# Feed-forward of a hybrid decoder block: up-projection by Strassen's seven half-size products, activations through DRAM, down-projection with half its weight held in SBUF

## The chip, the cores and the metric

One core of a Trainium2 chip runs the whole kernel. TensorE (PE), VectorE (DVE), ScalarE (ACT), GpSimd (POOL) and SyncE (SP, which here only issues DMAs) run side by side and wait for each other by semaphores. The metric is device time in microseconds for one execution.

## What is computed

A decoder block on 2048 positions of width 1024: an S5 state-space head group and eight stick-breaking attention heads, an output projection, cross-attention over 256 memory tokens, and a feed-forward of inner width 4096. The two parts that matter here:

```python
def block(qi, i):   # stick_breaking_attention, per block of 128 queries
    logits = einsum('bqhd,bkhd->bhqk', qi, k) * scale
    log_beta = log_sigmoid(logits)
    log_1m_beta = where(mask, log_sigmoid(-logits), 0.0)
    after = lax.cumsum(log_1m_beta, axis=3, reverse=True) - log_1m_beta
    w = where(mask, exp(log_beta + after), 0.0)
    return einsum('bhqk,bkhd->bqhd', w, v)
...
h = rmsnorm(x, g_mlp[l])                                   # (2048, 1024)
x = x + jnp.square(jax.nn.relu(h @ w_up[l])) @ w_down[l]    # w_up 1024 x 4096, w_down 4096 x 1024
```

All is float32. For the large products each operand is kept as a rounded part (hi, fp32r, made by ACT) and the rest (lo, made by DVE), and three matmuls, hi x hi, hi x lo and lo x hi, stand for one.

## The kernel before

`decoder_block` calls one function for each stage, and a barrier of all engines ends each.

**Feed-forward (`mlp`).** The rows are cut into 2 chunks of 1024 (`CHUNKS2`), the inner width into 16 blocks of 256 (`BLOCKS`, `FB`). For a chunk h^T (1024 x 1024) lies in SBUF as `ht_hi` and `ht_lo`. It is made by norm on DVE (`norm_x`), 8 transposes per tile of 128 rows on PE (`turn_h`), `high_h` on ACT and `low_h` on DVE. For each block `up` makes four units (two halves of rows by two tiles of 128 inner columns), each of 24 matmuls of 128x128 by 512 columns (lines 2687 to 2689). ACT takes Relu out of PSUM, DVE multiplies it by itself (line 2612), ACT rounds to `a_hi`, DVE subtracts to `a_lo`. `down` follows one block behind: 8 tiles of 128 rows, each of 12 such matmuls, 6 for each half of the output columns (lines 2703 to 2705), and DVE adds each tile from PSUM to `y` in SBUF (line 2595). The weights of a block come in one DMA of 1 MB each (`load_up`, line 2449, and `load_down`), into one buffer each (`up_raw`, `down_raw`), and are split by `split_up` and `split_down` on ACT and DVE. POOL only makes the identity matrix. At a chunk's end `boundary` finishes the last block and turns the tiles of the next chunk. Most of the blocks run in hardware loops (`Fori`).

The order on each engine is written out by hand: `program` runs prologue, up, down and boundary, and a `Tally` counts steps in a semaphore.

**Stick-breaking (`stick_breaking`).** Heads go in pairs. For each tile of 128 queries `score` (lines 796 to 799) makes the logits on PE, ACT the two sigmoids, DVE the running product (scan, line 740), POOL the weights (line 690), PE turns them (811) and multiplies by v (828). At the start SP runs `load_half(0, 0)`: q of both heads for 1024 positions (2 DMAs of 512 KB), hi and lo part of k, each twice (8 DMAs of 256 KB), then v. The first score waits for all ten.

## Time and profile before

| what | us |
|---|---|
| runs shown: median of 3 (lowest to highest) | 3311.54 (3311.31 to 3315.63) |
| the profiled execution's own time | 3312.09 |
| its span, first to last instruction | 3310.3 |
| feed-forward stage: first instruction to end of span | 1848.8 to 3310.3 |
| attention stage: first instruction to last score | 642.8 to 1174 |

"Busy" is the time in which an engine had an instruction under way. Matmuls overlap, so that one of 392 ns starts every 0.2267 us; that distance is the pace. "Idle before, releaser" is the time in which the engine stood still ahead of the instruction, and what ended it. PEclk is the granted clock of PE as a share of the full one; a mean share between the two levels says how long each of them held. The chain of work that ended last is followed back from the end of the span. In the names f_ is the feed-forward, a_ the attention, s_ the state-space stage, p_ the input projection.

### The profile page before, as it was taken

The numbers are of one execution on the slowest core, as the hardware profiler recorded it, in microseconds if no ns is written. First come the engines' busy times: TensorE is split into PE (matmuls) and PEld (weight loads), VectorE is DVE, ScalarE is ACT, GpSimd is POOL, SyncE is SP. The second block draws the span as 40 slices with busy tenths as digits, with TensorE's granted clock in tenths as the row PEclk, the third lists the DMA queues.
The fourth block names the chain that finished last, engine by engine and source line by source line (L and its number), as shares of the span: only waits on it lengthen the run. The fifth ranks groups of instructions, "written<-read, shape, count | busy, mean of one in ns | idle before, by whom it ended". The sixth has DMA issues, their size and how long they took to land. (4 is left out here: it accounts for less than half of the span.)

```text
span 3310.3 us, 42553 instructions
## 1 busy us (share of the span) xinstructions
PE 3008.5 (91%) x15810; PEld 2545.5 (77%) x15810; DVE 1717.8 (52%) x2404; ACT 1106.8 (33%) x1839; POOL 494.4 (15%) x397
## 2 busy tenths in 40 slices
PE   6999936599999969986999699999999999999998
PEld 5888824488988957764888588888887788888887
DVE  5333257587877855436565444444444544444444
ACT  4333215376766752213343221111111211111111
POOL 1212113455555532110000000000000000000000
PEclk9999967899999989997999899999999999999999
DMA  4232252362242033324222521111111411111111
GB/s 163 83 92 73 77 79 43 86 167 55 49 101 54 11 80 102 95 93 155 71 85 69 202 65 51 50 38 51 42 47 52 165 51 38 51 51 51 51 38 64
DMA packets 230220, 251.36 MB, mean 76 GB/s; under 512 B 107457, under 2 KB 181185, under 8 KB 230081
## 3 DMA queue, kind: packets, MB, share of 16 engines
q1 hardware_dynamic: 230096, 249.74, 25.8%
q8 instruction: 75, 1.23, 0.2%
q14 instruction: 49, 0.39, 0.0%
HBM read 189.79 MB, written 58.73 MB: 75 GB/s over the span
## 5 line engine op out<-in xcount | busy, mean ns | idle before, releaser
L2595 DVE TENSOR_TENSOR f_y<-f_ps_down,f_y 128x1024 f32<-128x1024 f32 x256 | 313.2, 1224 | 324.9 <-PE f_ps_down L2705 324.8
L2538 ACT ACTIVATE f_act_f<-f_ps_up 128x512 f32<-128x512 f32 x128 | 76.5, 598 | 1032.0 <-PE f_ps_up L2689 1032.0
L2687 PE MATMUL f_ps_up<-f_ht_hi,f_up_hi 128*128 128x512 f32 x1024 | 401.2, 392 | 6.4 <-DVE f_act_f L2612 6.4
L2703 PE MATMUL f_ps_down<-f_down_hi,f_a_hi 128*128 128x512 f32 x1024 | 400.4, 391 | 6.1 <-issue 6.1
L2688 PE MATMUL f_ps_up<-f_ht_lo,f_up_hi 128*128 128x512 f32 x1024 | 400.4, 391 | 0.0
L2689 PE MATMUL f_ps_up<-f_ht_hi,f_up_lo 128*128 128x512 f32 x1024 | 400.3, 391 | 0.0
L2705 PE MATMUL f_ps_down<-f_down_hi,f_a_lo 128*128 128x512 f32 x1024 | 400.0, 391 | 0.0
L2704 PE MATMUL f_ps_down<-f_down_lo,f_a_hi 128*128 128x512 f32 x1024 | 400.0, 391 | 0.0
L690 POOL TENSOR_TENSOR a_w<-a_on,a_left 128x640 f32<-128x640 f32 (+5 forms) x192 | 282.1, 1469 | 254.6 <-DVE a_left L740 114.6
L2612 DVE SCALAR_TENSOR_TENSOR f_act_f<-f_ps_up,f_act_f 128x512 f32<-128x512 f32 x128 | 88.5, 691 | 395.3 <-ACT f_act_f L2538 395.3
L828 PE MATMUL a_ps_y<-a_wt,a_v 128*96 128x128 f32 x2176 | 270.6, 274 | 5.2 <-DVE a_yt L763 5.2
L828 PEld LDWEIGHTS a_ps_y<-a_wt,a_v 128*96 128x96 f32 x2176 | 249.6, 164 | 5.8 <-issue 5.8
L740 DVE TENSOR_TENSOR_SCAN a_left<-a_ps_z,a_one 128x896 f32<-128x896 f32 (+7 forms) x128 | 207.3, 1620 | 77.5 <-ACT a_ps_z L702 75.9
L2687 PEld LDWEIGHTS f_ps_up<-f_ht_hi,f_up_hi 128*128 128x128 f32 x1024 | 193.6, 189 | 47.0 <-DVE f_ht_lo L2578 6.8
L2703 PEld LDWEIGHTS f_ps_down<-f_down_hi,f_a_hi 128*128 128x128 f32 x1024 | 193.3, 189 | 46.8 <-issue 6.7
L2689 PEld LDWEIGHTS f_ps_up<-f_ht_hi,f_up_lo 128*128 128x128 f32 x1024 | 193.4, 189 | 40.5
L2688 PEld LDWEIGHTS f_ps_up<-f_ht_lo,f_up_hi 128*128 128x128 f32 x1024 | 193.6, 189 | 40.2
L2705 PEld LDWEIGHTS f_ps_down<-f_down_hi,f_a_lo 128*128 128x128 f32 x1024 | 193.2, 189 | 40.4
L2704 PEld LDWEIGHTS f_ps_down<-f_down_lo,f_a_hi 128*128 128x128 f32 x1024 | 193.1, 189 | 40.2
L701 ACT ACTIVATE a_on<-a_ps_z 128x640 f32<-128x640 f32 (+5 forms) x192 | 148.8, 775 | 162.6 <-PE a_ps_z L799 120.8
L796 PE MATMUL a_ps_z<-a_k_hi,a_q 128*128 128x512 f32 (+3 forms) x392 | 145.3, 378 | 30.6 <-DMA a_k_lo<-k 22.7
L485 PE MATMUL p_acc<-p_w_hi,p_ht_hi 128*128 128x512 f32 x384 | 155.7, 405 | 2.7 <-DVE p_ht_lo L390 2.7
(352 smaller groups left out, 5505.9 us busy)
## 6 DMA issues: line engine op xcount, KB each, us to landing
f_up_raw<-in_w_up SPq DMA_DIRECT2D x32, 1024.0 KB, 5.3
f_down_raw<-in_w_down SPq DMA_DIRECT2D x32, 1024.0 KB, 4.8
p_xt<-in_x SPq DMA_DIRECT2D x16, 512.0 KB, 4.8
q<-p_qt SPq DMA_DIRECT2D x16, 512.0 KB, 3.2
k<-p_qt SPq DMA_DIRECT2D x16, 512.0 KB, 3.2
a_q<-q SPq DMA_DIRECT2D x16, 512.0 KB, 5.6
a_k_hi<-k SPq DMA_DIRECT2D x32, 256.0 KB, 8.4
...
```

The lines of the kernel that those rows point to most:

```text
L485: pe.matmul(out, ht_hi[b][:, k, rows], w_hi[:, k, cols], start=(k == 0), stop=False)
L690: pool.tensor_tensor(w[m % WS][:, 0:k1 - k0], on[m % ONS][:, 0:k1 - k0], left[a][i % 2][:, at + k0 + 1:at + k1 + 1], ALU.mult).then_inc(we ...
L701: act.activation(on[m % ONS][:, 0:k1 - k0], z, ACT.Sigmoid, scale=SCALE).then_inc(sig_on, 1)
L740: dve.tensor_tensor_scan(left[a][i % 2][:, at + k0:at + k1][:, ::-1], z_ps[m % 2][:, 0:k1 - k0][:, ::-1], one[:, 0:1].to_broadcast([P, k1 ...
L828: mm = pe.matmul(y_ps[a][0:TALL, 0:P], v[a][(2 * s + half) % 3][:, cols], wt[m % WTS][:, t, :], start=(first and t == 0), stop=(last and t ...
L2595: dve.tensor_tensor(y[:, t, :], down_ps[t % 2][:, :], y[:, t, :], ALU.add).then_inc(added.sem, 1)
L2687: pe.matmul(o, up_hi[:, k, cols], ht_hi[:, k, rows], start=(k == 0), stop=False)
L2688: pe.matmul(o, up_hi[:, k, cols], ht_lo[:, k, rows], start=False, stop=False)
L2689: mm = pe.matmul(o, up_lo[:, k, cols], ht_hi[:, k, rows], start=False, stop=(k == KC - 1))
L2703: pe.matmul(o, a_hi[par][:, s, rows], down_hi[:, s, cols], start=(s == 0), stop=False)
L2704: pe.matmul(o, a_hi[par][:, s, rows], down_lo[:, s, cols], start=False, stop=False)
L2705: mm = pe.matmul(o, a_lo[par][:, s, rows], down_hi[:, s, cols], start=False, stop=(s == S - 1))
```

## The change

**Up-projection.** A chunk of 1024 rows and a block of 256 inner columns, at depth 1024, is one product of 2 x 2 by 2 x 2 quarters. It is done with seven products of quarter operands (Strassen's scheme in Winograd's form) instead of eight: each of 12 matmuls of 128x128 by 512, into one PSUM bank. Their operands are quarters of W (A11 to A22) and of h (H11 to H22), or sums of them. For each block POOL makes the four weight sums S1 to S4, ACT rounds and DVE subtracts all seven weight operands; for each chunk the seven h operands (T1 to T4 among them, made by DVE for chunk 0 and by POOL for chunk 1) lie in SBUF as hi and lo, one buffer each. DVE puts the results together from PSUM (C11, U2, U3, C21, C22, U4, C12) in an order woven with its subtractions for the next block. ACT applies Relu, then Square, and SP stores the activations to a DRAM tensor `a` (4096 x 2048). There is one raw buffer for the up weights, as before. The norm of x goes to ACT, and g is multiplied in by DVE when it copies the turned tile from PSUM. The tiles of chunk 1 are turned in blocks 1 to 8, one each.

**Down-projection.** It starts after all 32 blocks. For each half of the output columns the whole depth of `w_down` (32 tiles, hi and lo) lies in SBUF; for each group of 512 rows the sum over the depth of 4096 stays in four PSUM banks, in two sets by turns. A step is one depth tile: 12 matmuls. Activations are loaded back, two depth tiles per 512 KB DMA, split by ACT and DVE into a ring of 3; in the first group of each half the weights are loaded and split beside them. `y` is added once per group. All 256 steps are written out.

**Attention's start.** The loads of the first pair's lower half are cut at column 512: ten loads of 0 to 511, then v, then ten loads of 512 to 1023. The first score waits for the first ten, query tile 4 for the second ten.

The diff, cut to its core:

```diff
-            load_half(0, 0)
+            def load_begin(cols, done_q, done_k):
+
+                for a in range(2):
+                    sp.dma_start(q2[a][:, cols].bitcast(F32), q_dram[a, :, cols]).then_inc(done_q, DMA)
+                    for dst, part in ((k2_hi[a][0], 0), (k2_lo[a][0], 1)):
+                        for copy in range(2):
+                            sp.dma_start(dst[copy * HEAD:(copy + 1) * HEAD, cols].bitcast(F32),
+                                         k_dram[a, part * HEAD:(part + 1) * HEAD, cols]).then_inc(done_k, DMA)
+
+            load_begin(slice(0, BANK), begin_loaded, begin_loaded)
+            for a in range(2):
+                sp.dma_start(v[a][0][:, 0:BLOCKS * HEAD // 2].rearrange("p (i d) -> p i d", d=HEAD),
+                             v_dram[0:HALF, a * HEAD:(a + 1) * HEAD].rearrange("(i p) d -> p i d", p=P)
+                             ).then_inc(v_loaded[0], DMA)
+            load_begin(slice(BANK, HALF), q_loaded[0], k_loaded[0])
             load_half(0, 1)
...
-                if i in (0, BLOCKS // 2) and first:
+                if s == 0 and i == 0:
+                    pe.wait_ge(begin_loaded, 10 * DMA)
+                elif i == (BANK // P if s == 0 else 0) or i == BLOCKS // 2 and first:
                     half = i // (BLOCKS // 2)
...
+        big = sb("big", [P, 35, 1024], F32R)
+        h_raw = sb("h_raw", [P, KC, ROWS])
+        w_raw = sb("w_raw", [P, 2, 1024])
+        w_sum = sb("w_sum", [P, 3, KH, P])
+        u2 = sb("u2", [P, BANK])
+        xr = sb("xr", [P, 4, 1024])
...
+        def hv(i, low):
+            return big[:, 4 * i + 2 * low:4 * i + 2 * low + 2, :].rearrange("p a (b q) -> p (a b) q", b=2)
+
+        def wv(i, low):
+            return big[:, 28 + i, low * BANK:(low + 1) * BANK].rearrange("p (k q) -> p k q", q=P)
...
+        W_SRC = {ONE: A11, SIX: S2, TWO: A12, SEVEN: S3, FIVE: S1, FOUR: A22, THREE: S4}
+        W_SUMS = {FIVE: 1, SIX: 2, SEVEN: 3, THREE: 4}
+        H11, H12 = h_raw[:, :KH, :BANK], h_raw[:, :KH, BANK:]
+        H21, H22 = h_raw[:, KH:, :BANK], h_raw[:, KH:, BANK:]
+        T3, T2, T4, T1 = H12, H11, H21, H12
+        H_SRC = {ONE: H11, SIX: T2, TWO: H21, SEVEN: T3, FIVE: T1, FOUR: T4, THREE: H22}
+        H_SUMS = {SEVEN: 1, SIX: 2, FOUR: 3, FIVE: 4}
...
+        BOUNDARY = {(BLOCKS - 1, 1): ONE, (BLOCKS - 1, 3): TWO, (BLOCKS - 1, 4): SIX, (BLOCKS - 1, 5): SEVEN,
+                    (BLOCKS - 1, 6): THREE, (BLOCKS, 0): FOUR, (BLOCKS, 2): FIVE}
+
+        def boundary_variant(b, slot, plain):
+            return None if plain else BOUNDARY.get((b, slot))
+
+        STEPS = [(half, g, k) for half in range(2) for g in range(GROUPS) for k in range(FF_TILES)]
...
             def load_up(b):
...
+                sp.dma_start(raw, w_up[:, b * FB:(b + 1) * FB].rearrange("(k p) f -> p k f", p=P)).then_inc(w_loaded, DMA)
...
+            def body(b, chunk):
+                if b < LAST:
+                    sp.wait_ge(w_low.sem, w_low.at(b, FOUR + 1))
+                    sp.wait_ge(w_summed.sem, w_summed.at(b, 4))
+                    load_up((b + 1) % BLOCKS)
+                if b == 0:
+                    load_x(TILES)
+                    load_x(TILES + 1)
+                if is_turning(b, False) and TILES + b + 1 < 2 * TILES:
+                    load_x(TILES + b + 1)
+                store_a(b, chunk, SQ11, 0, 0, 0)
+                if b == LAST:
+                    load_down(0)
+                    for i in range(4):
+                        sp.wait_ge(stored[i].sem, stored[i].at(BLOCKS - 1, DMA))
+                    load_a(0)
+                    load_down(1)
+                    load_a(1)
+                store_a(b, chunk, SQ21, 3, 1, 0)
+                store_a(b, chunk, SQ22, 2, 1, 1)
+                store_a(b, chunk, SQ12, 1, 0, 1)
...
+            def sum_one(b):
+                pool.wait_ge(w_loaded, b * DMA + DMA)
+                pool.wait_ge(w_low.sem, w_low.at(b - 1, FIVE + 1))
+                pool.tensor_tensor(S1, A21, A22, ALU.add).then_inc(w_summed.sem, 1)
+
+            def sum_two(b):
+                pool.wait_ge(w_summed.sem, w_summed.at(b, 1))
+                pool.wait_ge(w_low.sem, w_low.at(b - 1, THREE + 1))
+                pool.tensor_tensor(S2, S1, A11, ALU.subtract).then_inc(w_summed.sem, 1)
+
+            def sum_three(b):
+                pool.wait_ge(w_low.sem, w_low.at(b - 1, SEVEN + 1))
+                pool.tensor_tensor(S3, A11, A21, ALU.subtract).then_inc(w_summed.sem, 1)
+
+            def sum_four(b):
+                pool.wait_ge(w_low.sem, w_low.at(b, SIX + 1))
...
+            def high_w(b, i):
+                act.wait_ge(made.sem, made.at(b - 1, i + 1))
+                if i in W_SUMS:
+                    act.wait_ge(w_summed.sem, w_summed.at(b, W_SUMS[i]))
+                else:
+                    act.wait_ge(w_loaded, b * DMA + DMA)
+                act.activation(wv(i, 0), W_SRC[i], ACT.Copy).then_inc(w_high.sem, 1)
...
+            def activate(b, r, made_by, n):
+                act.wait_ge(combined.sem, combined.at(b, made_by))
+                act.activation(r, r, ACT.Relu).then_inc(relued.sem, 1)
+                act.wait_ge(relued.sem, relued.at(b, n))
+                act.activation(r, r, ACT.Square).then_inc(squared.sem, 1)
...
+            def body(b, plain=False):
+                more = plain or b < LAST
+                act.wait_ge(made.sem, made.at(b, ONE + 1))
+                act.wait_ge(combined.sem, combined.at(b - 1, C12))
+                act.activation(u2[:, :], PS_A, ACT.Copy).then_inc(one_copied.sem, 1)
+                if more:
+                    high_w(b + 1, ONE)
+                slot_end(b, 0, plain)
+                if more:
+                    high_w(b + 1, TWO)
+                slot_end(b, 1, plain)
+                activate(b, R11, C11, SQ11)
...
+            def high_a(n):
+                m = n // 2
+                act.wait_ge(a_loaded[m % 2], (m // 2 + 1) * DMA)
+                if n < RING:
+                    act.wait_ge(made.sem, made.at(LAST, FOUR + n + 1))
+                else:
+                    act.wait_ge(step_made, n - RING + 1)
+                act.activation(a_slot(n, 0), a_raw(m)[:, n % 2, :], ACT.Copy).then_inc(a_high, 1)
+
+            for n, (half, g, k) in enumerate(STEPS):
+                high_a(n)
+                if g == 0:
+                    high_down(half, k)
...
+            def body(b, plain=False):
+                more = plain or b < LAST
+                if more:
+                    low_w(b + 1, ONE)
+                slot_end(b, 0, plain)
+                dve.wait_ge(made.sem, made.at(b, TWO + 1))
+                dve.wait_ge(one_copied.sem, one_copied.at(b, 1))
+                dve.wait_ge(stored[0].sem, stored[0].at(b - 1, DMA))
+                dve.tensor_tensor(R11, PS_B, u2[:, :], ALU.add).then_inc(combined.sem, 1)
...
+            def add_group(group):
+                dve.wait_ge(y_loaded[group % 2], (group // 2 + 1) * 4 * DMA)
+                for t in range(4):
+                    dve.wait_ge(step_made, (group + 1) * FF_TILES)
+                    dve.tensor_tensor(y_tile(group, t), acc(group, t), y_tile(group, t), ALU.add).then_inc(added, 1)
...
+            def product(b, i, plain):
+                pe.wait_ge(w_low.sem, w_low.at(b, i + 1))
+                if not plain and b % BLOCKS == 0:
+                    pe.wait_ge(hv_low, b // BLOCKS * PRODUCTS + HV_ORDER.index(i) + 1)
+                o = OUT_BANK[i]
+                for k in range(KH):
+                    pe.matmul(o, wv(i, 0)[:, k, :], hv(i, 0)[:, k, :], start=(k == 0), stop=False)
+                    pe.matmul(o, wv(i, 0)[:, k, :], hv(i, 1)[:, k, :], start=False, stop=False)
+                    mm = pe.matmul(o, wv(i, 1)[:, k, :], hv(i, 0)[:, k, :], start=False, stop=(k == KH - 1))
+                mm.then_inc(made.sem, 1)
...
+            def body(b, plain=False):
+                pe.wait_ge(combined.sem, combined.at(b - 1, C21))
+                product(b, ONE, plain)
+                pe.wait_ge(combined.sem, combined.at(b - 1, U4))
+                product(b, TWO, plain)
+                if not plain and b == 0:
+                    for n in range(TILES - 2, TILES):
+                        turn_h(n)
+                pe.wait_ge(combined.sem, combined.at(b - 1, C12))
+                product(b, SIX, plain)
+                pe.wait_ge(combined.sem, combined.at(b - 1, U3))
+                product(b, SEVEN, plain)
+                pe.wait_ge(one_copied.sem, one_copied.at(b, 1))
+                product(b, FOUR, plain)
+                if is_turning(b, plain):
+                    turn_h(TILES - 1 + b)
+                pe.wait_ge(combined.sem, combined.at(b, C11))
+                product(b, FIVE, plain)
+                pe.wait_ge(combined.sem, combined.at(b, U2))
+                product(b, THREE, plain)
...
+            for n, (half, g, k) in enumerate(STEPS):
+                group = half * GROUPS + g
+                if k == 0:
+                    if group == 0:
+                        pe.wait_ge(h_copied, 2 * TILES)
+                    elif group == 1:
+                        pe.wait_ge(combined.sem, combined.at(LAST, C12))
+                    else:
+                        pe.wait_ge(added, (group - 1) * 4)
+                pe.wait_ge(a_low, n + 1)
+                if g == 0:
+                    pe.wait_ge(down_low, half * FF_TILES + k + 1)
+                for t in range(4):
+                    o = acc(group, t)
+                    rows = slice(t * P, (t + 1) * P)
+                    hi, lo = (a_slot(n, low)[:, rows] for low in range(2))
+                    pe.matmul(o, hi, w_slot(k, 0), start=(k == 0), stop=False)
+                    pe.matmul(o, hi, w_slot(k, 1), start=False, stop=False)
+                    mm = pe.matmul(o, lo, w_slot(k, 0), start=False, stop=(k == FF_TILES - 1))
+                mm.then_inc(step_made, 1)
```

## Rows read from the trace of the kernel before

**Rows 1.** The page, busy us (share of the span) and instructions of each engine

```profile
PE 3008.5 (91%) x15810; PEld 2545.5 (77%) x15810; DVE 1717.8 (52%) x2404; ACT 1106.8 (33%) x1839; POOL 494.4 (15%) x397
```

**Rows 2.** The page, chain that ended last, by line, share of the span

```profile
PE f_ps_up L2687 7%; PE f_ps_down L2703 7%; PE f_ps_up L2688 7%; PE f_ps_up L2689 7%; PE f_ps_down L2705 7%; PE f_ps_down L2704 7%; PE f_ps_th L2663 0%; DVE f_ht_lo L2578 0%; DVE f_xt L2571 0%; DMA f_g_row<-in_g_mlp 0%; ACT f_ht_hi L2515 0%; DVE f_y L2595 0%; DVE f_up_lo L2583 0%; DVE f_act_f L2612 0%; PE f_ps_down L2663 0%
```

**Rows 3.** Busy us by stretch (PE, PEld, DVE, ACT, POOL), clock, DMA share, GB/s

```profile
1848.80:1874.20 25.40, 8.29 (x40) 7.29 (x41) 16.25 (x24) 5.88 (x6) 0.46 (x2) 0.57 0.72 251
1874.20:1900.00 25.80, 22.48 (x101) 18.55 (x100) 9.77 (x10) 6.53 (x9) 0.00 (x0) 0.89 0.68 246
...
2000.00:2100.00 100.00, 100.00 (x443) 82.81 (x442) 45.70 (x48) 20.64 (x30) 0.00 (x0) 1.00 0.15 53
...
2557.00:2614.00 57.00, 46.55 (x218) 37.81 (x218) 33.80 (x31) 12.44 (x14) 0.00 (x0) 0.91 0.54 203
...
3305.10:3310.30 5.20, 0.19 (x1) 0.00 (x0) 1.23 (x1) 0.00 (x0) 0.00 (x0) 0.97 0.42 169
```

**Rows 4.** Groups of instructions, feed-forward: count, busy us, mean ns, idle before

```profile
L2687 PE MATMUL f_ps_up<-f_ht_hi,f_up_hi 128*128 128x512 f32 x1024 | 401.2, 392 | 6.4 <-DVE f_act_f L2612 6.4
...
L2595 DVE TENSOR_TENSOR f_y<-f_ps_down,f_y 128x1024 f32<-128x1024 f32 x256 | 313.2, 1224 | 324.9 <-PE f_ps_down L2705 324.8
...
L2612 DVE SCALAR_TENSOR_TENSOR f_act_f<-f_ps_up,f_act_f 128x512 f32<-128x512 f32 x128 | 88.5, 691 | 395.3 <-ACT f_act_f L2538 395.3
L2620 DVE TENSOR_TENSOR f_a_lo<-f_act_f,f_a_hi 128x512 fp32r<-128x512 f32 x128 | 87.5, 684 | 4.2 <-ACT f_a_hi L2546 4.2
L2546 ACT ACTIVATE f_a_hi<-f_act_f 128x512 fp32r<-128x512 f32 x128 | 79.6, 622 | 6.3 <-DVE f_act_f L2612 6.3
...
L2521 ACT ACTIVATE f_up_hi<-f_up_raw 128x1024 fp32r<-128x1024 f32 x64 | 67.4, 1053 | 0.0
```

**Rows 5.** Instructions in order: start us, us, engine, line [idle before]

```profile
2000.14 0.39 PE L2687 MATMUL f_ps_up<-f_ht_hi,f_up_hi 128*128 128x512 f32 x1
...
2013.74 0.39 PE L2703 MATMUL f_ps_down<-f_down_hi,f_a_hi 128*128 128x512 f32 x1
...
2013.94 0.60 ACT L2538 ACTIVATE f_act_f<-f_ps_up 128x512 f32<-128x512 f32 x1 [3.38 <-PE f_ps_up L2689]
```

**Rows 6.** Pieces of the chain that ended last: start us, us, what

```profile
2572.15 0.87 PE f_ps_th L2663 x8
...
3281.68 0.47 PE f_ps_down L2703
```

**Rows 7.** Instructions of DVE in order, feed-forward's opening and last block

```profile
1857.62 2.48 DVE L2571 SCALAR_TENSOR_TENSOR f_xt<-f_xt,f_stat,f_g_row 128x1024 f32<-128x1024 f32 x2
...
3286.29 1.22 DVE L2595 TENSOR_TENSOR f_y<-f_ps_down,f_y 128x1024 f32<-128x1024 f32 x1 [4.71 <-PE f_ps_down L2705]
```

**Rows 8.** Line 2449: SP's issue of the up weights, ns; landing, us

```profile
L2449 SPq DMA_DIRECT2D f_up_raw<-in_w_up x32: 368/368/1017, 1851.7 to 3172.1; - x32
...
DMA to landing us min/median/max: 5.1/5.3/10.3
```

**Rows 9.** DVE and POOL in order, state-space stage, 628 to 634 us

```profile
628.84 1.26 POOL L1011 TENSOR_TENSOR s_s_cos<-s_tables,s_sigma 128x510 f32<-128x510 f32 x1 [2.79 <-DVE s_sigma L1291]
629.20 1.44 DVE L1299 TENSOR_TENSOR s_s_sin<-s_tables,s_sigma 128x510 f32<-128x510 f32 x1
...
631.85 0.69 DVE L1299 TENSOR_TENSOR s_s_sin<-s_tables,s_sigma 128x510 f32<-128x510 f32 x1
631.95 1.71 POOL L1011 TENSOR_TENSOR s_s_cos<-s_tables,s_sigma 128x510 f32<-128x510 f32 x1 [1.85 <-issue]
```

**Rows 10.** Groups of POOL's instructions: a 128x512 product

```profile
L270 POOL TENSOR_TENSOR p_qn<-p_qn,p_gq_row 128x512 f32<-128x512 f32 x32 | 40.6, 1292 | 304.8 <-DVE p_qn L418 304.8
```

**Rows 11.** Instructions in order at attention's start

```profile
642.80 0.83 SPq L638 DMA_DIRECT2D a_q<-q  x2
...
660.45 0.44 PE L796 MATMUL a_ps_z<-a_k_hi,a_q 128*128 128x128 f32 x1 [22.73 <-DMA a_k_lo<-k]
```

**Rows 12.** Busy us by stretch after attention's start, columns as in rows 3

```profile
680.00:700.00 20.00, 19.87 (x154) 17.79 (x155) 18.45 (x22) 15.35 (x26) 13.21 (x8) 1.00 0.97 293
```

More of the change, by code:

```diff
@@ L2354, in mlp @@
     FB = 256
-    S = FB // P
     BLOCKS = D_FF // FB
-    HALVES = ROWS // BANK
-    U = HALVES * S
-    XT = 4
-    LAST = CHUNKS2 * BLOCKS - 1
+    ALL = CHUNKS2 * BLOCKS
+    LAST = ALL - 1
+    KH = KC // 2
+    ONE, TWO, SIX, SEVEN, FOUR, FIVE, THREE = range(7)
+    PRODUCTS = 7
+    HV_ORDER = (ONE, TWO, SIX, SEVEN, THREE, FOUR, FIVE)
+    FF_TILES = D_FF // P
+    GROUPS = SEQ // BANK
+    RING = 3
     with ExitStack() as ctx:
@@ L2384, in mlp @@
         ident = sb("ident", [P, P])
+        g_col = sb("g_col", [P, KC])
         stat = sb("stat", [P, 4, SEQ // P])
-        up_ps = [ps(f"up{i}", [P, BANK]) for i in range(2)]
-        down_ps = [ps(f"down{i}", [P, D_MODEL]) for i in range(2)]
-        th_ps = ps("th", [P, KC, P])
+        bank = [ps(f"bank{i}", [P, BANK]) for i in range(4)]
+        th_ps = [ps(f"th{i}", [P, KC, P]) for i in range(2)]
+        PS_A, PS_B, PS_C, PS_D = (b[:, :] for b in bank)
+        OUT_BANK = {ONE: PS_A, TWO: PS_B, SIX: PS_C, SEVEN: PS_D, FOUR: PS_A, FIVE: PS_B, THREE: PS_C}
@@ L2417, in turned_into @@
[L2417 to L2437 removed]
+        h_copied = sem("h_copied")
@@ L2505, in _ @@
+            sums(0)
+            sums(1)
+            for b in range(1, BLOCKS - 1):
+                sums(b + 1)
+            sum_heads(SEVEN)
+            sum_one(BLOCKS)
+            sum_two(BLOCKS)
+            sum_heads(SIX)
+            sum_three(BLOCKS)
+            sum_heads(FOUR)
+            sum_four(BLOCKS)
+            sum_heads(FIVE)
+            for b in range(BLOCKS, LAST):
+                sums(b + 1)
         @block.scalar
         def _(act):
-            for t in (up_high, down_high, relued, a_high):
+            for t in (w_high, one_copied, relued, squared):
@@ new lines, in low_h @@
+            def low_h(chunk, i):
+                dve.wait_ge(hv_high, chunk * PRODUCTS + HV_ORDER.index(i) + 1)
+                dve.tensor_tensor(hv(i, 1), H_SRC[i], hv(i, 0).bitcast(F32), ALU.subtract).then_inc(hv_low, 1)
+            for n in range(4):
+                copy_h(n)
+            low_h(0, ONE)
+            low_w(0, ONE)
+            copy_h(4)
+            low_h(0, TWO)
+            low_w(0, TWO)
+            copy_h(5)
+            low_w(0, SIX)
+            low_w(0, SEVEN)
+            copy_h(6)
@@ new lines, in _ @@
+            low_w(0, FOUR)
+            low_w(0, FIVE)
+            copy_h(7)
+            low_w(0, THREE)
+            dve.wait_ge(h_copied, TILES)
+            dve.tensor_tensor(T3, H22, H12, ALU.subtract).then_inc(h_summed[0], 1)
+            dve.wait_ge(h_summed[0], H_SUMS[SEVEN])
+            dve.wait_ge(hv_low, HV_ORDER.index(ONE) + 1)
+            dve.tensor_tensor(T2, T3, H11, ALU.add).then_inc(h_summed[0], 1)
+            low_h(0, SIX)
+            low_h(0, SEVEN)
+            dve.wait_ge(h_summed[0], H_SUMS[SIX])
@@ new lines, in _, with slot_end @@
+            dve.wait_ge(hv_low, HV_ORDER.index(TWO) + 1)
+            dve.tensor_tensor(T4, H21, T2, ALU.subtract).then_inc(h_summed[0], 1)
+            low_h(0, THREE)
+            dve.wait_ge(hv_low, HV_ORDER.index(SEVEN) + 1)
+            dve.tensor_tensor(T1, H22, T2, ALU.subtract).then_inc(h_summed[0], 1)
+            for i in (FOUR, FIVE):
+                low_h(0, i)
+            def slot_end(b, slot, plain):
+                i = boundary_variant(b, slot, plain)
+                if i is not None:
+                    low_h(1, i)
```

563 lines of the change are left out of this document (294 added, 269 removed).

## The prediction

> **What bounds the kernel now.** I read the shares of the page first, then the chain that ended last, then stretches of the feed-forward, then single instructions. TensorE (PE) is busy 91% of the span [rows 1], and the six feed-forward matmul groups alone hold 43% of it in the chain [rows 2]. In a stretch amid the feed-forward PE is busy 100.00 of 100 us at granted clock 1.00, while DVE is busy 45.70 and ACT 20.64 [rows 3]. So there only fewer or faster matmuls help. Sixty matmuls pass from 2000.14 to 2013.74, 0.2267 us each [rows 5]. The stage runs from 1848.8 to the end of the span at 3310.3: 1461.5 us. Its 6144 matmuls take 1392.8 of them; 68.7 are opening, chunk boundary and end [rows 3].
>
> **Fewer products.** Up-projection: 32 blocks of 7 products of 12 matmuls, 2688, where there were 3072; down: 256 steps of 12, 3072 as before. 5760 x 0.2267 = 1305.8 us, 87.0 less. Every matmul keeps its form (128x128 by 512), so I take the pace unchanged, in the down part too. One product lasts 2.72 us, one block 19.04. Everything else the change does costs time, or is to be hidden in those 19.04 us.
>
> **One steady block.** Let t = 0 be the first matmul of product ONE. Per block DVE has 7 subtractions of 0.684 and 8 sums of 0.691, 10.3 us; ACT 15 instructions of about 0.62, 9.4 us [rows 4]; POOL 4 sums of 1.27 (a 128x512 product took 1.292) [rows 10], 5.1 us. Each fits. What may not fit is the loop through the single raw weight buffer. SP issues load_up(b+1) behind the last store of block b-1, which waits for its last Square. THREE's result is seen 0.2 us after its end (PE 2013.74, ACT 2013.94) [rows 5]; sum 0.69, Relu and Square 1.3, two issues 0.45: the load is issued at 2.6. Landing takes a median 5.3, least 5.1, most 10.3 [rows 8]. Now 256 KB stores go just ahead; at 251 GB/s [rows 3] one takes 1 us, so I estimate L = 6.2. ACT's and DVE's first conversions for the next block stand in their queues ahead of this block's sums, so until the data lands both queues stand still; PE misses nothing until FIVE at 13.6, which needs C11.
> After landing at Z, POOL's four sums meet DVE's subtractions. Where both read SBUF they take turns: DVE's L1299 takes 0.69 alone, but 1.44 when it starts 0.36 us into a POOL sum, ending 0.54 after it; a POOL sum started while DVE runs takes 1.71 instead of 1.26 [rows 9]. Laid out in turns: subtraction ONE ends at Z+1.9, C11 Z+2.5, subtraction TWO Z+3.65, SIX Z+5.35, SEVEN Z+7.2, C21 Z+7.85. From there ACT: Relu+Square 1.3, conversion FIVE 0.5, Relu+Square 1.3, conversion THREE 0.5, Relu+Square 1.3, then the issues 0.45: the next load can go at Z+13.2. The loop is L + 13.2 = 19.4 us, against PE's 19.04. It costs 0.4; I take 0.5 in each of the 21 blocks that have nothing else, 10.5 us. Bounds: nothing (if L is below 5.8), or 1.8 if one more POOL sum of 1.27 falls into the loop.
> The Trainium skill (SBUF — State Buffer, Who interferes with whom) speaks against this use of POOL: a VectorE instruction with two SBUF inputs and a GpSimd one that reads SBUF exclude each other for the whole instruction. By that rule the loop is the 19.4 above; without it the same chain would be L + 12.0 = 18.2, hidden. The pairs at 629 and 632 us agree with the rule.
>
> **Opening.** Up to the first norm nothing changes much: 8.8 us (DVE 1857.62) [rows 7]; the nine small loads take the place of one of g. Then DVE must do 8 copies of 1.22, 7 weight subtractions of 0.69, 4 sums and 7 subtractions of 2048 columns before block 0 can end. A 2048-column instruction is 0.69 + 3 x 0.53 = 2.3 (0.53 is the difference between 1024 and 512 columns) [rows 4]. That is 39.9 us. First norm and transposes 3.1, DVE's waits for ACT and PE by a schedule laid out by hand 12.7, then a subtraction and C11 1.4 and products FIVE and THREE 5.4: block 1 starts at 71.4, and I add 3 for matmuls at the low clock. After a gap a step of 12 takes 4.4 us (3281.68 to the add at 3286.29, less 0.2) instead of 2.72 [rows 6, 7], 1.7 more. 74.4 less block 0's own 19.0 leaves 55.4. If the waits halve it is 48.
>
> **Turning the second chunk** in blocks 1 to 8: 0.87 of transposes each [rows 6], as before the change too. Here PE waits between FOUR and FIVE for the norm, which stands in ACT's queue behind the conversions of loaded weights: norm ends about 14.6, FOUR ended at 13.6. 0.87 + 1.0 = 1.9 each, 15.2. The loop's 0.4 is hidden in it.
>
> **Chunk boundary**, blocks 15 and 16. Each of the 7 operands of h has one buffer, so it is replaced between its product in block 15 and that in block 16: 7 x (2.0 ACT, twice a 1024-column one, + 2.3 DVE), and POOL's three chained sums of about 5 us. DVE's load over the two blocks is 2 x 10.3 + 16.1 = 36.7 of 38.1, in a fixed order with POOL's sums. ONE(16) waits for C21(15), which is behind the operand conversions: near t = 25 instead of 19, 5.7 lost. TWO and SIX lose some more; FOUR(16) waits for its operand, which ACT makes only after load_up(17) has landed, 6.6; FIVE about 4.3. In all 19.5, plus 3 for the low clock, plus 5 for turns with POOL: 27.5. Bounds: 12, if the waits overlap, and 40.
>
> **Into down, and down itself.** After the last product: sum, Relu, Square, then conversion and subtraction of the first activation and weight slots, 4.3 us, plus 1.7 at the low clock: 6. Then in each 2.72 us step ACT has one or two instructions of 0.62, DVE one or two of 0.68; with weights DMA brings 1 MB in 5.44 us, 190 GB/s, below the 251 of [rows 3], and five steps of lead less 2.7 of conversions leave 7.9 us for a landing. The four sums of a group run beside three ready steps. I cost the reading of activations at nothing; the cover is the ring of 3. If the landing took 10.3, the 32 loads with weights would lose up to 2.4 each, 77 us: unlikely, since they go two at a time. 3072 matmuls stay 696.4. The store and load instructions that pass SP at a group change (8 x 0.4) lie in that lead too. End: four adds of 0.65, issue and landing, 6.0 where it was 5.2 [rows 3].
>
> Sum for the stage: 1305.8 + 55.4 + 15.2 + 10.5 + 27.5 + 6 + 6 = 1426.4, against 1461.5: 35.1 saved. Of 87.0 more than half is given back.
>
> **Attention's start.** PE's first score starts at 660.45, after waiting for DMA; loads are issued from 642.80 [rows 11]. That is 3.15 MB of q and k in 17.65 us, 178 GB/s. The change lets the first four query tiles start after half: 8.8 us earlier. The second half, behind v, makes 3.67 MB or 20.6 us, about when tile 4 wants it (its score started some 11 us after the first). From 680 PE is full (19.87 of 20) [rows 12], so a lead stays. Against it: ten more issues of about 0.6 us on SP ahead of the upper half, at a DMA share of 0.97. Bounds -2 to 8.8; I take 7, nearest to the landing row.
>
> **Forecast.** 35.1 + 7 = 42.1. The profiled execution took 3312.09 (span 3310.3, 1.8 around it), 0.55 above the median 3311.54 of the runs shown: 3312.1 - 42.1 = 3270.
>
> **Rivals.**
> A. The weight loop is hidden and the boundary's waits overlap: 10.5 + 15.5 less, 3244. For it: 5.3 as median landing, and DVE and ACT over half idle. Against: stores now go just ahead of each load.
> B. The weight loop is 1.3 us longer (one more turn with POOL): 21 x 1.3 = 27, 3297; with half of it 3283. For it: the pairs [rows 9] and the fixed order of POOL's sums.
> C. Slower than before: the loop sets the pace outright. With a period P the loss is 21 x (P - 19.04) + 8 x (P - 20.9); my sum without it saves 52.6, so from P = 21.4 the kernel is no faster, and from 21.6 (L = 8.4) it is slower by over 0.2%. At the longest landing seen, 10.3, P is 23.5: 3374. For it: single buffer, and each queue in order. Against: that 10.3 had four 512 KB loads ahead of it.
> D. The attention part does nothing, since the saturated DMA only passes the wait on: 3277. For it: DMA share 0.97 afterwards [rows 12].
>
> **Chances.** Forecast, 3258 to 3280: 0.42; A 0.20; B 0.22 (3283 to 3300); C 0.06; D 0.10. The bounds of the opening and boundary reach 20 either way. 3242 to 3296 leaves out C and the ends of A and B, about 2 in 10. A measurement here can tell about 0.2% (6.6 us) from no change. Faster 0.91, within 0.03, slower 0.06.
>
> **What would show it.** Steps right: 2688 up matmuls at 0.2267; a steady block of 19.0 to 19.6 (more: B or C, and then PE's idle time sits before the product that needs C11 or C12); landing of the up weights near 6; DVE subtractions of more than 0.69 beside POOL sums; about 75 us from the stage's start to block 1; a gap of 20 to 35 around blocks 15 and 16; a down part of 696 without gaps; first score about 9 us after the stage's start. Wrong: gaps inside the down steps, a pace above 0.227, or a first score as late as before.

## The result, and the profile after

The changed kernel takes 3293.38 us (median of 5 runs, 3291.99 to 3293.99) against 3311.54 before (3307.62 to 3315.63): ratio 0.9942, interval 0.9928 to 0.9957. It is 18.2 us faster. I had forecast 41.5 us, a time of 3270 with 3242 to 3296 as range. The time lies near the upper end of the range, beside rival B and not beside the forecast.

The page of the kernel after: busy time of each engine, and by line the chain that ended last.

```profile
PE 2946.1 (90%) x15426; PEld 2485.3 (76%) x15426; DVE 1696.0 (52%) x2566; ACT 1362.9 (41%) x2301; POOL 705.0 (21%) x529
...
PE f_ps_th L3001 4%; PE f_ps_th L3003 4%; PE f_ps_th L3002 4%; PE f_ps_bank L3002 4%; PE f_ps_bank L3001 4%; PE f_ps_bank L3003 4%; DMA f_w_raw<-in_w_up 2%; PE f_ps_bank L2957 1%; PE f_ps_bank L2959 1%; PE f_ps_bank L2958 1%; ACT f_xr L2713
```

In [rows 2] the up-projection held 21% of the chain and DMA nothing. Now the down part still holds its share (21% before, six groups of 4% now), but the up-projection's matmuls (L2957 to L2959) hold 1% each: the chain runs beside them, through the load of raw up weights (2%, some 66 us) and ACT's Relu (L2713). This is what a loop through another engine looks like in a chain. The stage starts at 1841.8 and the span ends at 3291.5. Busy time of its stretches, columns as in [rows 3]: opening, blocks 1 to 8 (which turn the second chunk), plain blocks 9 to 13, the chunk boundary, plain blocks 17 to 31, and down:

```profile
1841.80:1911.70 69.90, 36.49 (x149) 30.43 (x150) 49.08 (x49) 31.23 (x33) 13.54 (x10) 0.69 0.33 109
1911.70:2103.20 191.50, 172.06 (x737) 141.04 (x737) 93.97 (x122) 87.22 (x139) 47.05 (x32) 0.94 0.35 106
2103.20:2201.70 98.50, 97.33 (x427) 79.66 (x426) 53.22 (x70) 45.00 (x78) 29.54 (x20) 1.00 0.33 104
2224.60:2290.70 66.10, 45.53 (x157) 35.12 (x158) 49.68 (x37) 32.56 (x41) 27.43 (x11) 0.79 0.21 64
2290.70:2582.70 292.00, 288.58 (x1261) 235.31 (x1259) 155.70 (x204) 135.16 (x234) 82.73 (x56) 1.00 0.36 111
2587.00:3285.00 698.00, 698.00 (x3072) 577.57 (x3072) 230.01 (x346) 192.82 (x317) 0.00 (x0) 1.00 0.42 140
```

Most of the idle time beyond opening and boundary is in the second row: 19.4 us without a matmul in 8 blocks, and a granted clock of 0.94. What PE waited for there (total us, times, longest us), and then the instructions of one such block in order:

```profile
PE f_ps_th L2945 <- ACT f_xr L2692: 19.4, 8, 2.9
```

```profile
1963.39 0.38 SPq L2527 DMA_DIRECT2D f_w_raw<-in_w_up  x1
...
1970.30 1.29 POOL L2631 TENSOR_TENSOR f_w_sum<-f_w_raw 128x512 f32<-128x512 f32 x1 [17.75 <-DMA f_w_raw<-in_w_up]
...
1970.32 1.15 ACT L2700 ACTIVATE f_big<-f_w_raw 128x512 fp32r<-128x512 f32 x2 [6.27 <-DMA f_w_raw<-in_w_up]
...
1975.62 1.13 ACT L2692 ACTIVATE f_xr<-f_xr,f_stat 128x1024 f32<-128x1024 f32 x1
...
1976.80 1.97 PE L2945 MATMUL f_ps_th<-f_ident,f_xr 128*128 128x128 f32 x8 [2.52 <-ACT f_xr L2692]
...
1978.42 0.78 PE L2957 MATMUL f_ps_bank<-f_big 128*128 128x512 f32 x1
...
1987.59 0.38 SPq L2527 DMA_DIRECT2D f_w_raw<-in_w_up  x1
```

The load issued at 1963.39 is in at 1970.30. ACT converts two weight blocks, makes four more instructions and then, at 1975.62, the norm (L2692); PE, idle for 2.52 us, turns the tile from 1976.80 to 1978.42 (1.62 us), and product FIVE begins, slow at first. The next load goes out at 1987.59, 17.3 us after the landing. The next block therefore finds its weights as late as this one did: the delay is not absorbed, it sets the period, 24.2 us here.

The same links in a plain block: load issued, landed, a subtraction of DVE, POOL's third sum, and the next issue:

```profile
2352.25 0.38 SPq L2527 DMA_DIRECT2D f_w_raw<-in_w_up  x1
2358.96 1.15 ACT L2700 ACTIVATE f_big<-f_w_raw 128x512 fp32r<-128x512 f32 x2 [6.68 <-DMA f_w_raw<-in_w_up]
...
2359.63 1.22 DVE L2816 TENSOR_TENSOR f_big<-f_w_raw,f_big 128x512 fp32r<-128x512 f32 x1 [8.29 <-ACT f_big L2700]
...
2361.95 1.74 POOL L2640 TENSOR_TENSOR f_w_sum<-f_w_raw 128x512 f32<-128x512 f32 x1
...
2371.97 0.38 SPq L2527 DMA_DIRECT2D f_w_raw<-in_w_up  x1
```

L is 6.7, the rest 13.0, the period 19.7. Over all 32 loads the landing has (min/median/max):

```profile
DMA to landing us min/median/max: 6.1/6.6/8.8
```

### The profile page after: what moved, and what is told of

The parts are those of the page before. It is cut to its first block and busy times, and to the rows that moved or that the text cites. A ratio compares the mean times of both kernels' runs of the same rounds, so it can differ in the third digit from the quotient of the medians.

```text
span 3291.5 us, 42858 instructions
## 1 busy us (share of the span) xinstructions
PE 2946.1 (90%) x15426; PEld 2485.3 (76%) x15426; DVE 1696.0 (52%) x2566; ACT 1362.9 (41%) x2301; POOL 705.0 (21%) x529
## 5 line engine op out<-in xcount | busy, mean ns | idle before, releaser
L2917 DVE TENSOR_TENSOR f_big<-f_h_raw,f_big 128x512 fp32r<-128x512 f32 x256 | 177.0, 691 | 463.3 <-ACT f_big L2792 463.3
L2957 PE MATMUL f_ps_bank<-f_big 128*128 128x512 f32 x896 | 361.1, 403 | 43.8 <-DVE f_big L2820 19.8
L2792 ACT ACTIVATE f_big<-f_h_raw 128x512 fp32r<-128x512 f32 x256 | 161.7, 632 | 497.9 <-PE f_ps_bank L3003 259.7
L2958 PE MATMUL f_ps_bank<-f_big 128*128 128x512 f32 x896 | 356.5, 398 | 0.0
L2959 PE MATMUL f_ps_bank<-f_big 128*128 128x512 f32 x896 | 356.0, 397 | 0.0
L2957 PEld LDWEIGHTS f_ps_bank<-f_big 128*128 128x128 f32 x896 | 173.9, 194 | 89.2 <-issue 25.1
L2816 DVE TENSOR_TENSOR f_big<-f_w_raw,f_big 128x512 fp32r<-128x512 f32 x96 | 103.5, 1078 | 244.3 <-ACT f_big L2700 244.3
L3001 PE MATMUL f_ps_th<-f_big 128*128 128x512 f32 x512 | 200.0, 391 | 4.0 <-DVE f_big L2912 4.0
L2959 PEld LDWEIGHTS f_ps_bank<-f_big 128*128 128x128 f32 x896 | 172.8, 193 | 37.3
L2958 PEld LDWEIGHTS f_ps_bank<-f_big 128*128 128x128 f32 x896 | 173.6, 194 | 35.6
L3003 PE MATMUL f_ps_th<-f_big 128*128 128x512 f32 x512 | 199.8, 390 | 0.0
L3002 PE MATMUL f_ps_th<-f_big 128*128 128x512 f32 x512 | 199.8, 390 | 0.0
L3001 PE MATMUL f_ps_bank<-f_big 128*128 128x512 f32 x512 | 199.2, 389 | 0.0
L3002 PE MATMUL f_ps_bank<-f_big 128*128 128x512 f32 x512 | 199.2, 389 | 0.0
L3003 PE MATMUL f_ps_bank<-f_big 128*128 128x512 f32 x512 | 199.2, 389 | 0.0
```

Source lines behind the costliest of these rows:

```text
L2792: act.activation(a_slot(n, 0), a_raw(m)[:, n % 2, :], ACT.Copy).then_inc(a_high, 1)
L2917: dve.tensor_tensor(a_slot(n, 1), a_raw(n // 2)[:, n % 2, :], a_slot(n, 0).bitcast(F32), ALU.subtract).then_inc(a_low, 1)
L2957: pe.matmul(o, wv(i, 0)[:, k, :], hv(i, 0)[:, k, :], start=(k == 0), stop=False)
L2958: pe.matmul(o, wv(i, 0)[:, k, :], hv(i, 1)[:, k, :], start=False, stop=False)
L2959: mm = pe.matmul(o, wv(i, 1)[:, k, :], hv(i, 0)[:, k, :], start=False, stop=(k == KH - 1))
L3001: pe.matmul(o, hi, w_slot(k, 0), start=(k == 0), stop=False)
```

## The experiments

**The theory.** The up-projection is paced by one loop: load, landing, conversions, Relu and Square, store, next load. In plain blocks it is slightly longer than PE's 19.04 us; in turning blocks it also passes through the norm, the transposes and product FIVE, and is 24 us. **Rivals:** the norm's place in ACT's queue alone costs the gap; POOL's turns with DVE do; or the landing is slow for a reason of its own. I measured block lengths from one copy of product ONE (ACT, out of PSUM) to the next: the mean of blocks 1 to 8 for a turning block, of blocks 17 to 30 for a plain one. "Boundary" is blocks 15 and 16 together, in us:

| kernel | median | ratio (interval) | turning block | plain block | boundary |
|---|---|---|---|---|---|
| after | 3293.38 | 0.9942 (0.9928 to 0.9957) | 23.94 | 19.6 | 66.1 |
| load two stores earlier | 3247.27 | 0.9804 (0.9787 to 0.982) | 20.01 | 19.04 | 64.1 |
| norm earlier | 3268.98 | 0.9869 (0.9851 to 0.9887) | 20.68 | 19.6 | 65.7 |
| small POOL sums | 3258.89 | 0.9838 (0.9821 to 0.9854) | 21.38 | 19.04 | 64.6 |
| a quarter of each load | 3244.42 | 0.9799 (0.9782 to 0.9815) | 19.99 | 19.04 | 61.0 |
| before, attention's part alone | 3304.72 | 0.9979 (0.997 to 0.9988) | - | - | - |
| load and norm earlier | 3247.53 | 0.9807 (0.9792 to 0.9822) | 19.96 | 19.04 | 62.4 |
| load earlier, boundary sums on DVE | 3239.37 | 0.9784 (0.9769 to 0.9799) | 19.96 | 19.04 | 58.0 |
| all of these, and a new order | 3234.32 | 0.9768 (0.9753 to 0.9783) | 19.88 | 19.04 | 52.4 |

Ratios are to the kernel before, run beside each.

**Load earlier.** SP issues the load for block b+2 behind the second of block b's four stores, no longer behind the fourth:

```diff
-                if b < LAST:
-                    sp.wait_ge(w_low.sem, w_low.at(b, FOUR + 1))
-                    sp.wait_ge(w_summed.sem, w_summed.at(b, 4))
-                    load_up((b + 1) % BLOCKS)
...
                 store_a(b, chunk, SQ21, 3, 1, 0)
+                if b + 2 < ALL:
+                    sp.wait_ge(w_low.sem, w_low.at(b + 1, FOUR + 1))
+                    sp.wait_ge(w_summed.sem, w_summed.at(b + 1, 4))
+                    load_up((b + 2) % BLOCKS)
```

> The changed kernel with one edit on SP: the up weights of a block are loaded as soon as their buffer is free, two stores earlier in SP's queue, instead of behind the last store of the block before. Loop theory (the pace is set by the round trip load, conversions, last Square, last store, next load: 13.1 us after landing in a plain block, 17.3 in a turning block, plus 6.6 of landing): with the load off the round trip a plain block falls from 19.66 to 19.04 and a turning block from 23.9 to about 19.9, FOUR(16) no longer waits for its load; 3293.4 - 13 - 31 - 5 = about 3245. Turns theory (POOL and DVE excluding each other is itself the limit, wherever the load lands): plain blocks stay at 19.5 or more, total above 3275. Transposes theory (turning blocks are long by PE's transposes and the low clock alone): turning blocks stay above 22, total about 3278.

It came as the loop said: 3247.27. Turning blocks are 19.04 + 1.0, plain ones 19.04. Two stretches, turning blocks and plain blocks 17 to 31, columns as above:

```profile
1913.50:2073.60 160.10, 159.73 (x738) 132.64 (x737) 91.71 (x122) 88.89 (x139) 46.89 (x32) 1.00 0.43 130
...
2251.80:2535.00 283.20, 283.20 (x1251) 234.52 (x1250) 148.77 (x203) 146.21 (x232) 82.33 (x56) 1.00 0.36 112
```

PE has one gap of 0.37 us left in them, and the clock is 1.00 in both. The loads themselves are no faster, yet it doesn't matter, since each has a lead:

```profile
DMA to landing us min/median/max: 5.7/7.0/8.8
```

No work was taken away: one DMA issue stands elsewhere in SP's queue, and that is worth 46.1 us, more than twice what the whole change brought.

**Norm earlier.** ACT's norm of a turning block goes ahead of the conversions that wait for loaded weights:

```diff
                 act.activation(u2[:, :], PS_A, ACT.Copy).then_inc(one_copied.sem, 1)
+                if is_turning(b, plain):
+                    norm_x(TILES - 1 + b)
...
-                if is_turning(b, plain):
-                    norm_x(TILES - 1 + b)
                 if more:
                     high_w(b + 1, FOUR)
```

> The changed kernel with one edit on ACT: in the turning blocks the norm stands at the start of the block, ahead of the conversions that wait for the load. Loop theory: the transposes, FIVE and THREE leave the round trip, a turning block falls from 23.9 to about 20.1 (landing 6.9 plus 13.2), plain blocks stay at 19.66; 3293.4 - 30 = about 3263. Transposes theory: nothing moves, 3293, since PE still has 8 transposes per turning block. Rival in between, that x's loads slow the landing: less than 10 us gained.

The turning block falls to 20.68 (I had 20.1). ACT makes the copies at the end later than those at the start in this run; by PE's own first matmuls of ONE it is 20.41. PE no longer waits ahead of the transposes in any block, and the clock stays at 1.00. What is left is a wait ahead of FIVE, for C11, of up to 0.8 us:

```profile
1987.83 0.50 PE L2957 MATMUL f_ps_bank<-f_big 128*128 128x512 f32 x1 [0.76 <-DVE f_xr L2866]
```

That is the wait of the plain blocks, which don't change. The total misses by 6 us, of which the turning blocks explain 3 to 5. So the norm's place matters, but only inside the loop; what it does outside is seen below.

**Small sums.** POOL's four weight sums are left to 8 of their 128 columns, the rest of the sums stays zero:

```diff
-                pool.tensor_tensor(S1, A21, A22, ALU.add).then_inc(w_summed.sem, 1)
+                pool.tensor_tensor(S1[:, :, 0:8], A21[:, :, 0:8], A22[:, :, 0:8], ALU.add).then_inc(w_summed.sem, 1)
```

> The changed kernel, but each of POOL's four weight sums covers 8 of 128 inner columns (the rest stays zero, so the up-projection is not what the reference computes); everything else, waits too, as it is. It takes POOL's turns away from DVE. Loop theory with my pricing of the turns (1.2 us of them in the round trip): plain blocks fall to 19.04 (round trip 6.6 + 12.0 = 18.6), turning blocks by 1.1 or so, about 22 us in all: 3271. If the turns cost nothing: 3293. If they were the main part of the loss in turning blocks: those fall to 20 and the total to about 3250.

```profile
1963.71 0.25 POOL L2643 TENSOR_TENSOR f_w_sum<-f_w_raw 128x32 f32<-128x32 f32 x1
...
1963.85 0.69 DVE L2819 TENSOR_TENSOR f_big<-f_w_raw,f_big 128x512 fp32r<-128x512 f32 x1 [8.50 <-ACT f_big L2703]
...
1968.61 1.09 PE L2948 MATMUL f_ps_th<-f_ident,f_xr 128*128 128x128 f32 x8 [1.20 <-ACT f_xr L2695]
```

DVE's subtraction is back at 0.69 and PE's gap is 1.20 instead of 2.52. The turning block lost 2.6 us where I had allowed 1.2. The gap accounts for just that 1.2 (in the mean 1.20 where it was 2.43). The other 1.4 is PE's clock: with the shorter gap the granted clock stays at 1.00, and transposes and FIVE take 1.35 us less; more on this below. This run takes away the turns and also POOL's own 1.3 us a sum, on which ACT's conversions of the sums wait, and it can't say which of the two gave what. It doesn't speak against the loop: POOL's sums are links of it.

**A quarter of each load.** From the second block on only 256 KB of the 1 MB of raw up weights are loaded, so three quarters of them are those of the first block:

```diff
-                    load_up((b + 1) % BLOCKS)
+                    load_part((b + 1) % BLOCKS)
```

> The changed kernel, but after the first block only a quarter of the raw up weights is loaded anew (256 KB for 1 MB; the rest stays as it was, so the up-projection is not the reference's). It shortens the landing alone, from 6.6 to perhaps 4. Loop theory: plain blocks 19.04, turning blocks shorter by exactly as much as the landing (23.9 - 2.6 = 21.3), 3293.4 - 13 - 21 = about 3259. If the landing is not in the round trip: 3293 and no block changes.

```profile
DMA to landing us min/median/max: 2.8/3.1/3.8
```

The landing fell by 3.5 us (I had expected a landing of 4) and the turning block by 4.0, down to where PE alone sets it, and the total with it to 3244.42 (I had 3259). Here too 1.4 of the 4.0 are transposes and FIVE at a clock of 1.00. A load that starts no earlier but ends 3.5 us sooner repairs the same gap as one that starts earlier. So it isn't the place of the norm as such, nor the turns, that cost: it is the length of the round trip, by whichever link one shortens it.

**Attention's part alone**, put into the kernel before: `load_begin` and PE's wait for it, the feed-forward as before.

> The kernel before, with the attention part of the change alone (the first pair's lower half loaded in two pieces). My term was 7 us: 3311.5 - 7 = 3304.5, first score about 6 to 7 us earlier after the stage's start than before, and that lead kept to the end of the stage. Rival: the saturated DMA passes the wait on to tile 4 or to the upper half, and the total stays within 2 us of before.

3304.72 against 3312.57 beside it, ratio 0.9979: 7 us, between 4 and 10 (the two medians are 7.9 apart). Loads and first score, here and in the changed kernel:

```profile
642.10 0.35 SPq L664 DMA_DIRECT2D a_q<-q  x1
...
653.20 0.45 PE L813 MATMUL a_ps_z<-a_k_hi,a_q 128*128 128x128 f32 x1 [16.21 <-DMA a_k_lo<-k]
```

```profile
644.14 0.35 SPq L664 DMA_DIRECT2D a_q<-q  x1
...
654.86 0.45 PE L813 MATMUL a_ps_z<-a_k_hi,a_q 128*128 128x128 f32 x1 [15.80 <-DMA a_k_lo<-k]
```

From the first issue to the first score it was 17.65 us [rows 11]; it is 11.1 and 10.72. The lead is kept: the feed-forward starts 1198.8 us after the attention's first load with this part alone, where it was 1206.0.

**Load and norm earlier together.**

> The early load and the early norm together. Loop theory: with the load early the norm no longer ends after FOUR, so its place is worth nothing more: 3247 as with the early load alone, turning blocks 19.9. Rival, that the norm's place has a cost of its own (ACT's order): 2 to 8 us less than the early load alone.

3247.53, the time of the load alone within the noise of either. The 24 us that the norm's place could give (second experiment) are gone once the load has a lead. This separates the norm's place as a cause by itself from a link in the loop.

**Boundary sums on DVE**, with the early load. Three of the four 2048-column sums of h move from POOL to DVE, each right behind the subtraction that frees its operand:

```diff
                 if i is not None:
                     low_h(1, i)
+                    dve.wait_ge(hv_low, PRODUCTS + HV_ORDER.index(i) + 1)
+                if i == ONE:
+                    dve.wait_ge(h_summed[1], H_SUMS[SEVEN])
+                    dve.tensor_tensor(T2, T3, H11, ALU.add).then_inc(h_summed[1], 1)
```

> Early load, and at the chunk boundary the three operand sums T2, T4 and T1 made by DVE (2.3 us each) instead of POOL (4.6 each, during which a DVE subtraction of 0.69 was seen to take 4.7). Turns theory for the boundary: DVE gives up 4 waits of 4 us and takes on 7 us of work, so blocks 15 and 16 fall from 64.1 to about 59 and the total from 3247 to 3242. If what counts is only the order of DVE's and ACT's queues, DVE's 7 us come on top: 3250 or more.

The boundary takes 58.0 instead of 64.1. What went, first with the early load alone, then here:

```profile
2200.60 4.61 POOL L2663 TENSOR_TENSOR f_h_raw<-f_h_raw 128x2048 f32<-128x2048 f32 x1 [2.90 <-DVE f_big L2824]
...
2200.98 4.77 DVE L2820 TENSOR_TENSOR f_big<-f_w_sum,f_big 128x512 fp32r<-128x512 f32 x1
```

```profile
2197.47 2.29 DVE L2861 TENSOR_TENSOR f_h_raw<-f_h_raw 128x2048 f32<-128x2048 f32 x1
...
2200.41 0.68 DVE L2817 TENSOR_TENSOR f_big<-f_w_sum,f_big 128x512 fp32r<-128x512 f32 x1
```

DVE's 0.69 us subtraction, started 0.38 us into POOL's sum, ends 0.54 us after it: it stood for 4.1 us. That happens three times at the boundary (4.77, 4.75, 4.70), 12.2 us of DVE. Doing the sum itself costs DVE 2.29.

**All of it, and a new order.** The early load, the early norm and the sums on DVE; besides, operands are made in the order in which they are needed and come free: THREE's conversion last, TWO's a slot later.

```diff
-    HV_ORDER = (ONE, TWO, SIX, SEVEN, THREE, FOUR, FIVE)
+    HV_ORDER = (ONE, TWO, SIX, SEVEN, FOUR, FIVE, THREE)
-        BOUNDARY = {(BLOCKS - 1, 1): ONE, (BLOCKS - 1, 3): TWO, (BLOCKS - 1, 4): SIX, (BLOCKS - 1, 5): SEVEN,
-                    (BLOCKS - 1, 6): THREE, (BLOCKS, 0): FOUR, (BLOCKS, 2): FIVE}
+        BOUNDARY = {(BLOCKS - 1, 1): ONE, (BLOCKS - 1, 4): TWO, (BLOCKS - 1, 5): SIX, (BLOCKS - 1, 6): SEVEN,
+                    (BLOCKS, 0): FOUR, (BLOCKS, 1): FIVE, (BLOCKS, 3): THREE}
```

> Early load, early norm, operand sums on DVE, and another order of the operand conversions: THREE last (also in the opening), and at the boundary TWO's conversion behind C21 instead of ahead of it, since ONE(16) waits for C21. Queue-order theory: ONE(16) starts some 4 us earlier, FIVE(16) has its operand two products earlier, the opening ends 2.3 earlier; total about 3235. If the conversions are simply too much work for two blocks, the waits move to TWO and SIX and the total stays at that of the sums on DVE.

3234.32 us, 0.9768 of the kernel before: the fastest version here. The longest of PE's gaps at the boundary; the changed kernel had these two and four more, 22.4 us in all:

```profile
2252.37 0.80 PE L2957 MATMUL f_ps_bank<-f_big 128*128 128x512 f32 x1 [8.19 <-DVE f_xr L2886]
...
2261.51 0.79 PE L2957 MATMUL f_ps_bank<-f_big 128*128 128x512 f32 x1 [4.20 <-DVE f_u L2893]
```

and this one has these four, 9.4 us in all:

```profile
2200.16 0.50 PE L2966 MATMUL f_ps_bank<-f_big 128*128 128x512 f32 x1 [0.53 <-DVE f_u L2881]
...
2209.61 0.62 PE L2966 MATMUL f_ps_bank<-f_big 128*128 128x512 f32 x1 [3.27 <-DVE f_u L2902]
...
2223.59 0.76 PE L2966 MATMUL f_ps_bank<-f_big 128*128 128x512 f32 x1 [3.91 <-DVE f_big L2821]
...
2232.55 0.47 PE L2966 MATMUL f_ps_bank<-f_big 128*128 128x512 f32 x1 [1.69 <-DVE f_big L2821]
```

## Why the prediction was right and wrong

The span fell by 18.8 us (3310.3 to 3291.5), 7.0 of them ahead of the feed-forward. The stage took 1449.7 us where my sum said 1426.4. The 23.3 us between them, by the terms of the sum:

| term | predicted | measured | difference |
|---|---|---|---|
| opening, to block 1 | 74.4 | 69.9 | -4.5 |
| turning blocks 1 to 8 | 8 x 20.94 | 8 x 23.94 | **+24.0** |
| blocks 9 to 14 | 117.2 | 121.3 | +4.1 |
| boundary, 15 and 16 | 65.6 | 66.1 | +0.5 |
| blocks 17 to 31 | 293.1 | 292.0 | -1.1 |
| into down, and down | 702.4 | 702.3 | -0.1 |
| end | 6.0 | 6.4 | +0.4 |

**The step that failed is the turning of the second chunk**, the term "0.87 + 1.0 = 1.9 each": it was 4.9 each. The mechanism named there was right: PE waits for the norm, which stands behind conversions of loaded weights. Both sizes in the term were too small. First, the gap. The norm's end at 14.6 fits the landing of before, 5.3 [rows 8], and not the 6.2 that I had estimated for the kernel after; with 6.2 the gap is 1.9 and not 1.0. Measured, in the block shown, are a load issued 2.9 after the block's start, a landing of 6.9 and a norm that ends at 16.2; the gap is 2.4 in the mean. Secondly, I priced the transposes at 0.87 [rows 6] and put nothing for PE's clock behind the gap. They took 0.85 to 1.62, 1.3 in the mean, and FIVE's twelve matmuls 1.0 more than 2.72. 2.4 + 1.3 + 1.0 = 4.7 of the measured 23.94 - 19.04 = 4.9.

That it is the clock, and not the gap as such, one of the eight blocks shows: the seventh. PE waits there as long as elsewhere, but the granted clock stays at 1.00; the transposes take 0.85, FIVE 0.13 more than 2.72, and the block 22.63 us, where the other seven average 24.13. First the transposes of the block shown above and of the seventh, busy time and clock, then the seventh's own start:

```profile
1976.80:1980.00 3.20, 3.20 (x12) 2.91 (x13) 1.83 (x3) 1.73 (x3) 0.08 (x1) 0.50 0.11 26
2072.70:2076.40 3.70, 3.70 (x20) 3.19 (x21) 1.53 (x3) 1.73 (x3) 0.00 (x0) 1.00 0.16 60
```

```profile
2072.70 1.10 PE L2945 MATMUL f_ps_th<-f_ident,f_xr 128*128 128x128 f32 x8 [2.45 <-ACT f_xr L2692]
...
2073.55 0.47 PE L2957 MATMUL f_ps_bank<-f_big 128*128 128x512 f32 x1
```

So the low level of the clock cost the seven blocks 1.5 us each in the mean, and with smaller gaps (1.20 us in the mean with the small sums) it stayed away.

Thirdly, I took the loop and the turning as two things ("the loop's 0.4 is hidden in it"). In a turning block the round trip itself runs through the norm, the transposes, FIVE and THREE, because the stores of FIVE's and THREE's results stand ahead of the next load in SP's queue: 6.9 + 17.3 = 24.2. The sum lacks no further term for it, since the gap was charged in each of the eight blocks; what I didn't see is that all of this loss hangs on when the load is issued. The early load shows it: 20.01, with the transposes at 0.79 and no gap but one.

**The opening** is 4.5 shorter than forecast: DVE waited 10.0 us between its first copy and C11 where I had 12.7, and from C11's end to block 1 it was 6.8 us, 1.4 more than two products, where I had added 3 for the low clock.

**The steady block** was right in mechanism and size: L 6.7 where I had 6.2, the rest 13.0 where I had 13.2, a period of 19.6 to 19.7 where I had taken 19.54. (I had counted 8 sums of DVE, where a block has 7, and 15 instructions of ACT, where it has 16; both fit all the same.) PE's wait sits before the product that needs C11, as foretold; DVE's subtractions take up to 1.4 us beside POOL's sums (0.69 alone), and POOL's sums 1.6 to 1.75 (1.3 alone). The Trainium skill (SBUF — State Buffer, Who interferes with whom) states that a VectorE instruction with two SBUF inputs and a GpSimd one that reads SBUF exclude each other, so that the second to issue waits until the first is finished. The trace agrees; at the boundary, with the early load, still more plainly with 4.77 us beside a sum of 4.61.

**Blocks 9 to 14** are 4.1 us longer, 3.3 of them through block 14 (22.85 from copy to copy; PE itself stands for 2.38 us ahead of TWO, at its end). The first of the h sums falls there, and with it a subtraction:

```profile
2218.28 5.05 POOL L2655 TENSOR_TENSOR f_h_raw<-f_h_raw 128x2048 f32<-128x2048 f32 x1
...
2219.40 4.49 DVE L2816 TENSOR_TENSOR f_big<-f_w_raw,f_big 128x512 fp32r<-128x512 f32 x1
```

I had the sums' length ("about 5 us") but only as a lump of 5 us for turns, and none of it in block 14. With the load earlier the sum falls at the same place and a subtraction is held as long, yet PE has no wait there and block 14 takes 18.94:

```profile
2179.83 4.60 POOL L2659 TENSOR_TENSOR f_h_raw<-f_h_raw 128x2048 f32<-128x2048 f32 x1
...
2180.53 4.46 DVE L2820 TENSOR_TENSOR f_big<-f_w_sum,f_big 128x512 fp32r<-128x512 f32 x1
```

**The boundary's** total, 28.0 lost against 27.5, is right more by luck than by its parts: I had 5 us for turns with POOL, and DVE stood for 12.1 (4.73, 4.75 and 4.70 instead of 0.69). Of PE's waits I had 5.7 for ONE(16), 6.6 for FOUR and 4.3 for FIVE; measured are 8.2, 5.9 and 1.2, and 4.2 for TWO. The run with the sums on DVE shows what the turns were worth, 6.1 us. The reordered one gave 5.7 more, but it has the early norm too, with which the boundary was 1.7 shorter by itself (62.4 for 64.1). Bounds of 12 and 40 were fair.

**The down part** went as forecast: 698.00 busy of 698, gap and slow start before it 5.9 against 6. Reading activations from DRAM cost nothing; they land in 3.7 us (median):

```profile
f_h_raw<-a SPq DMA_DIRECT2D x128, 512.0 KB, 3.7
```

**Attention's start** gave the 7 us that I took. The first score comes 10.7 us after the first issue, not the 8.8 that half of 17.65 makes, and 6.9 earlier than before. Rival D is out, by its own run. **The rivals:** A is out for this kernel (boundary as forecast, plain blocks not hidden), though with the load moved its half on the weight loop holds: plain blocks take 19.04. The boundary still loses 26.0 us then, not 12. B, by its time, is near the result, but not by its mechanism: plain blocks lost 0.6, not 1.3 more. C had the right form, a loop that sets the pace, but one period P for all blocks; it is 19.6 to 19.7 in the plain ones and 23.9 in the turning ones, where the round trip is another. What C forecast, a kernel slower than before, is out.

**What stays open:** how much of the 34.5 us that the small sums gave came from the turns and how much from POOL's own time; why the landing rose from 5.3 us to 6.6, which no run isolates; and why PE still waits 3.3 and 3.9 us in the best version's boundary, which was not followed further.
